# Forgetting attention: output product of one query tile joined to the scores of a later one, transposes and norm sums in other slots

## What is computed

```python
def block(inp):                       # one block of 128 queries
    q_b, c_b, start = inp
    logits = (jnp.einsum('bqhd,bkhd->bhqk', q_b, kf)
              + c_b[..., None] - c_k[:, :, None, :])
    q_pos = start + jnp.arange(Q_BLOCK)
    logits = jnp.where(key_pos[None, :] <= q_pos[:, None], logits, -jnp.inf)
    return jnp.einsum('bhqk,bkhd->bqhd', jax.nn.softmax(logits, axis=-1), vf)
...
o_fox = rms_norm(o_fox, fox_norm[i].reshape(FOX_HEADS, FOX_DH)).reshape(B, L, FOX_WIDTH)
h = h + jnp.concatenate([o_gla, o_fox], axis=-1) @ w_out[i]
```

## Time and profile before

| | before |
|---|---|
| median of 3 runs | 2259.5 us |
| profiled execution, span | 2257.8 us |
| PE busy | 2237.6 us (99%) |
| VectorE busy | 1411.1 us (62%) |
| ScalarE busy | 1049.8 us (46%) |
| chain that ended last | PE 93%, VectorE 3%, ScalarE 2% |
| granted TensorE clock | 0.999 of full |

### The profile page before, as it was taken

One profiled execution on the slowest core, in us unless ns is written; L12 is line 12 of the kernel. 1 busy time (PEld: TensorE's weight loads), 2 busy tenths in 40 slices (PEclk: granted clock), 3 DMA queues, 4 the chain that ended last, 5 costly groups with the idle time before them and its releaser, 6 DMA issues.

```text
span 2257.8 us, 39364 instructions
## 1 busy us (share of the span) xinstructions
PE 2237.6 (99%) x15807; PEld 2024.5 (90%) x15807; DVE 1411.1 (62%) x2601; ACT 1049.8 (46%) x1963; POOL 118.6 (5%) x203
## 2 busy tenths in 40 slices
PE   9999999999999999999999999999999999999998
PEld 7798999999997898999899888978899888898997
DVE  5356576759743465667689566869455455863664
ACT  5356554447633465544377443223244444552652
POOL 3001010000000001100000010101000000000001
PEclk9999999999999999999999999999999999999999
DMA  6545676245433436732355262767711122443651
GB/s 216 165 124 152 177 194 182 100 141 174 136 103 117 120 110 151 184 110 96 111 175 166 88 182 78 191 187 201 212 67 57 66 94 93 153 157 115 182 166 51
DMA packets 97112, 313.01 MB, mean 139 GB/s; under 512 B 13809, under 2 KB 17811, under 8 KB 95907
## 3 DMA queue, kind: packets, MB, share of 16 engines
q1 hardware_dynamic: 84627, 220.93, 29.6%
q0 software_dynamic: 11584, 88.25, 16.7%
q10 hardware_dynamic: 720, 1.31, 0.2%
HBM read 308.32 MB, written 86.02 MB: 175 GB/s over the span
## 4 chain that ended last, share of the span: by engine, by line
PE 93%; DVE 3%; ACT 2%; issue 1%; DMA 0%; POOL 0%; SPq 0%; ACTq 0%; DVEq 0%; POOLq 0%
PE G L1427 58%; PE G L1464 15%; PE G L1537 7%; PE X L1464 3%; PE X L1749 1%; PE X L1704 1%; PE X L1831 1%; PE X L1727 1%; DVE wL L2423 1%; PE X L1815 1%; PE X L1532 1%; ACT wH L1884 1%; PE X L1800 1%; PE X L1427 1%; PE X L1787 0%
## 5 line engine op out<-in xcount | busy, mean ns | idle before, releaser
L1884 ACT ACTIVATE wH<-raw 128x512 fp32r<-128x512 f32 (+3 forms) x693 | 475.0, 704 | 468.2 <-PE G L1427 386.9
L2423 DVE TENSOR_TENSOR wL<-raw,wH 128x512 fp32r<-128x512 f32 (+3 forms) x693 | 538.2, 788 | 240.2 <-ACT wH L1884 236.8
L1427 PE MATMUL G<-aH,wH 128*128 128x264 f32 (+2 forms) x2000 | 503.1, 317 | 2.0 <-DVE aL L2436 1.5
L1427 PE MATMUL G<-aH,wL 128*128 128x264 f32 (+2 forms) x2000 | 481.7, 306 | 0.0
L1427 PE MATMUL G<-aL,wH 128*128 128x264 f32 (+2 forms) x2000 | 481.2, 306 | 0.0
L1427 PEld LDWEIGHTS G<-aH,wH 128*128 128x128 f32 x2000 | 324.6, 189 | 28.2 <-issue 6.1
L1427 PEld LDWEIGHTS G<-aH,wL 128*128 128x128 f32 x2000 | 322.6, 188 | 17.2
L1427 PEld LDWEIGHTS G<-aL,wH 128*128 128x128 f32 x2000 | 322.6, 188 | 14.2 <-issue 0.2
L1464 PE MATMUL G<-seven,wH 128*128 128x256 f32 (+2 forms) x960 | 177.5, 284 | 1.6 <-DVE wL L2423 1.5
L2582 DVE TENSOR_TENSOR hT<-G,hT 128x528 f32<-128x528 f32 (+1 forms) x83 | 58.0, 699 | 183.4 <-PE G L1427 183.4
L1464 PEld LDWEIGHTS G<-seven,wH 128*128 128x128 f32 x960 | 148.0, 188 | 3.8 <-issue 3.0
(11 more groups left out here) (407 smaller groups left out, 3916.4 us busy)
## 6 DMA issues: line engine op xcount, KB each, us to landing
raw<-weights SPq DMA_DIRECT2D x195, 512.0 KB, 3.5
weight_sums<-weights POOLq DMA_DIRECT2D x72, 704.0 KB, 6.4
raw<-weight_sums SPq DMA_DIRECT2D x160, 256.0 KB, 2.9
raw<-weights SPq DMA_DIRECT2D x48, 704.0 KB, 4.0
raw<-weights SPq DMA_DIRECT2D x121, 256.0 KB, 2.8
weight_sums<-weight_sums POOLq DMA_DIRECT2D x24, 704.0 KB, 5.2
weight_sums<-weights POOLq DMA_DIRECT2D x24, 448.0 KB, 4.9
raw<-weights SPq DMA_DIRECT2D x12, 384.0 KB, 5.5
```

Source lines behind the costliest of these rows:

```text
L1427: done = e.matmul(m.pair(i)[0:M, bank, 0:n], a[:, k, 0:M], b[:, kx, lo - t0:lo - t0 + n], start=(k == 0 and c == 0), stop=(k == nk - 1 and ...
L1884: e.activation(m.high(i)[:, c], m.raw(i)[:, c], ACT.Copy).then_inc(s.w_hi, 1)
L2423: e.tensor_tensor(m.low(i)[:, c], m.raw(i)[:, c], m.high(i)[:, c].bitcast(F32), ALU.subtract).then_inc(s.w_lo, 1)
```

## The change

The body of the loop over w is laid out anew, and `RATE_FOX` goes from 0.8 to 0.64. `fo`(w−2) moves from the third slot of w to its first, directly ahead of `fs`(w). The first `yield` is skipped for w = 0. `ft`(w−1, 0) keeps the second slot, with `nsq` ahead of it for i = 2. `ft`(w−1, 1) moves to the third slot; for i = 2 `nsum` 0 stands ahead of it. The fourth slot holds `nsum` 1 (i = 2, so one w earlier than before) or `ft`(w−1, 2) (i = 1), then `fmeta`, `ftail` and `fn`(w, 1) as before. The extra slots that these steps had are gone, and so is the separate `nsum` 1 behind the loop.

```diff
-RATE_STATE, RATE_OUT, RATE_FOX, RATE_INDEX, RATE_HEADS = 0.5, 0.75, 0.8, 0.33, 0.62
+RATE_STATE, RATE_OUT, RATE_FOX, RATE_INDEX, RATE_HEADS = 0.5, 0.75, 0.64, 0.33, 0.62
@@ bg() in attention(l), for w in range(18) @@
                 if w < 16:
                     while ("fq", l, p) not in done:
                         yield "blocked"
+                if 2 <= w:
+                    step("fo", l, w - 2)
+                if w < 16:
                     step("fs", l, w)
                     if i == 1 and 1 <= p < 3:
                         step("sums", l, 2 * p + 2)
                         step("sums", l, 2 * p + 3)
                     if i == 4:
                         done.add(("pair", p))
-                yield
+                if w:
+                    yield
+                if i == 2 and p:
+                    step("nsq", l, p - 1)
                 if 1 <= w < 17:
                     step("ft", l, w - 1, 0)
                 yield
-                if i == 3 and p:
-                    step("nsum", l, p - 1, 1)
-                    yield
-                if 2 <= w:
-                    step("fo", l, w - 2)
+                if i == 2 and p:
+                    step("nsum", l, p - 1, 0)
                 if w < 16:
                     step("fn", l, w, 0)
-                yield
                 if 1 <= w < 17:
                     step("ft", l, w - 1, 1)
+                yield
+                if i == 2 and p:
+                    step("nsum", l, p - 1, 1)
+                if i == 1 and p:
+                    step("ft", l, w - 1, 2)
                 if i == 3 and w < 16:
                     step("fmeta", l, w)
                     if w == 10:
...
                 if w < 16:
                     step("fn", l, w, 1)
                 yield
-                if i == 1 and p:
-                    step("ft", l, w - 1, 2)
-                    yield
-                if i == 2 and p:
-                    step("nsq", l, p - 1)
-                    yield
-                    step("nsum", l, p - 1, 0)
-                    yield
-            step("nsum", l, 3, 1)
-            yield
             step("ftail", l, 3)
             done.add(("mix", 7))
```

## The result

| | before | after |
|---|---|---|
| median of 6 runs | 2259.47 us (2258.88 to 2259.78) | 2266.55 us (2265.74 to 2267.49) |
| ratio to before, 95% interval | | 1.0032 [1.0022, 1.0042] |
| profiled execution, span | 2257.8 us | 2265.1 us |
| granted TensorE clock, whole run | 0.999 | 0.998 (in all six runs) |

The change makes the kernel slower by 7.1 us, 0.32%. The forecast was 2268.7 us.

The account below looks back on a forecast made before the run. TensorE, busy 99% of the 2257.8 us span, was taken as the bound. −5.6 (joins) + 15.6 (`ft` waits) + 1.8 (dry) − 2.6 (old waits) = +9.2 us, giving 2268.7 us; range 2254 to 2276.

Parts of the forecast that it names:

- Part 1: `fo` joined to `fs`, 14 times a layer: each saves one re-entry and one entry, 0.20 us; 5.6 us in all.
- Part 3: `ft`(w−1,1) comes sooner after `fs`(w) and waits for its copy queued behind the exponentials: 7.8 us a layer, 15.6 in two.
- Part 4: Foreground runs dry before `fs`(3), so `fo`(1) waits for the copy of `ft`(1,1): 0.9 us a layer, 1.8 in two.
- Part 5: Old PE waits in the attention stretch go: 1.3 us a layer, 2.6 in two.
- `fo`(7) behind its copy: `fo`(7), one step behind `ft`(·,2), comes after 1.1 us against about 1.0 for the copy, so no wait.
- a join does nothing: Rival: each join gives 0.09 us or less while the waits come: 2271.8 us; chance 0.56 together with the forecast.
- Part 2: The other joins, `nsum` and `ft` (all full-array), cost or save zero, bounds −0.1 to +0.1 us for each of 8.
- the 0.09 behind a transposition: The foreground step after a transpose group takes 0.82 us instead of 0.73, put down to its own weight loads.
- joins win: Rival: ScalarE keeps up, no wait at `ft`, −6.4 us: 2253.1 us; chance 0.15.
- only the floor is left: Rival: foreground pieces on ScalarE mostly fall elsewhere, `ft` waits 5.4 us in place of 15.6: 2258.5 us; chance 0.22.
- the backlog: Rival: a late `ft` also delays other copies and VectorE's minima come late, +16.3 us: 2275.8 us; chance 0.07.
- The two layers behave alike, so I work one out and double it: Forgetting attention stretch: 134.30 us in either layer, clock granted in full, so one layer's terms were doubled.

Follow-up runs that it names:

- runs 1: Kernel before, old slots and rate, with only `fo`(w−2) moved directly ahead of `fs`(w): 2263.33 us.
- 11: run 9 with the `pair` mark one w earlier, RATE_FOX 0.66, and `fo` back in the third slot for i = 3 and 4: 2257.26 us.
- run 9: Changed kernel with `ft`(w−1, 1) in the fourth slot for i = 2, 3, 4 and foreground pieces held back from `fs`(w) to `ft`(w−1, 0): 2255.07 us.
- run 8: Changed kernel with `fs`(w) ahead of `fo`(w−2) and `ft`(w−1, 1) in the fourth slot for i = 2, 3, 4: 2259.28 us.
- run 4: Changed kernel with `ft`(w−1, 1) moved from the third slot to the fourth, except for i = 1: 2258.30 us.
- run 5: Changed kernel with the foreground's pieces held back between `fs`(w) and `ft`(w−1, 0), PE's order the same: 2259.11 us.
- run 2: Changed kernel with `ft`(w, 0) in the fourth slot of its own w and `ft`(w−1, 1) in the second: 2273.75 us.
- Run 3: Changed kernel with the copies of `ft`(·, 0) to PT made by VectorE instead of ScalarE: 2273.16 us.
- run 6: Changed kernel with the joined pair turned round, `fs`(w) first and `fo`(w−2) directly behind it: 2264.10 us.

## Why the prediction was right

The direction, the place and, within 2.2 us, the time were right. By the steps of the prediction, us per layer, measured by distances in layer 0:

| term | predicted | measured |
|---|---|---|
| Part 1, 14 joins | −2.8 | −2.8 |
| Part 3, waits at `ft` | +7.8 | +6.9 |
| Part 3, w = 3 / 7 / 11 | 1.46 / 1.46 / 1.94 | 1.46 / 1.56 / 2.16 |
| Part 4, dry stretch | +0.9 | +0.9 |
| Part 5, old waits | −1.3 | −2.3 |
| `fo`(7) behind its copy | 0 | +0.4 |

**Part 1** holds: the tail of `fo` stays, re-entry and entry go. By distances a join is worth 0.20 us in after, 0.18 in runs 1 and 11, 0.19 in run 9. The rival that a join does nothing falls, and run 8 against run 4 shows where it would nearly hold: with an untiled product in between. What Part 2 put at zero is not measured by itself; it is in these figures. The reason that it gives for the 0.09 behind a transposition, weight loads, no run here shows.

**Part 3** holds in its mechanism, which run 5 isolates without changing PE's order, and run 2 from the other side. Of its terms w = 4, 8, 9 and 12 were too large (0.21, 0.50, 0, 0.40 against 0.34, 0.82, 0.49, 0.58): each was the old order's lag carried over, with a guess at the pieces that fall between. Which of those failed I did not trace for each. The rivals that joins win, or that only the floor is left, fall with it; the backlog, 11 us a layer, did not come either.

**Part 4** is exact. PE's timeline of after:

```profile
150.16 0.52 PE L1724 MATMUL X<-ident,Sb 128*128 128x128 f32 x3
151.35 0.88 PE L1746 MATMUL X<-PT,fv 128*64 128x128 f32 x12 [0.67 <-ACT PT L2282]
```

1.19 us from start to start, where three transposes take 0.25 with foreground behind them: 0.94.

**Part 5** was mis-sized. I took the 1.3 us that the view of waits lists for before; by distances it was 2.3, as delays without a listed wait (0.75 at w = 11 in place of 0.60, and several of 0.1 to 0.4) count too.

Sum: −2.8 + 6.9 + 0.9 − 2.3 + 0.4 = +3.1 a layer, 6.2 in two, where 9.2 was predicted. The landmarks give 2.6 for layer 0. One yardstick for both kernels (at each entry, the distance less the usual one) gives 2.5 us of waits in before and 8.0 in after, 5.4 more without rounding; since the layer grows by 2.6, the joins and all that Part 2 moved are left with 2.8, 0.20 a join. So the half microsecond lies in the sizes of single waits in the table. Another 0.5 us arises between the two stretches (+2.39 to +2.85), and what makes it is open.

One step failed outright: "The two layers behave alike, so I work one out and double it". Layer 0 cost 2.6 us and layer 1 4.3, because in layer 1 TensorE's clock fell behind a wait, and no term had the clock in it. The measured 7.3 us of the span come nearer to the forecast than the terms do only because of these 1.6 us; that nearness is luck.

## What to carry to other kernels

Two pieces of PE work that are tiled otherwise than the bulk were worth joining for their entry and re-entry, 0.2 us a pair here, where they really touch: a full-array product at the seam takes more than half of it back. Before moving one, count the distance of every dependent pair in PE time against the chain it must cover, with all that stands in the in-order queue ahead of the copy, whatever engine has it; here the waits at `ft` were 6.9 us a layer against 2.8 for the joins. When such an order is changed, keep the distance (a later slot) and clear the queue (no background pieces between producer and copy): 2255.1 us instead of 2266.6, and 2259.4 before.

## What the runs showed of the hardware that I had not expected

The extra cost in layer 1 is TensorE's clock. Windows of after around `ft` at w = 11, layer 1 (PEclk is the column ahead of DMA share and GB/s):

```profile
868.00:871.80 3.80, 3.80 (x34) 3.24 (x30) 3.77 (x9) 1.71 (x4) 0.00 (x0) 1.00 0.87 141
871.80:874.20 2.40, 0.43 (x5) 0.34 (x4) 1.01 (x5) 1.95 (x6) 0.47 (x1) 1.00 0.39 77
...
874.60:877.90 3.30, 3.30 (x18) 3.30 (x16) 1.74 (x4) 1.08 (x2) 0.01 (x1) 0.51 0.96 245
```

and PE's timeline there:

```profile
873.89 0.63 PE L1724 MATMUL X<-ident,Sb 128*128 128x128 f32 x4 [1.97 <-ACT PT L2282]
...
875.44 0.64 PE L1424 MATMUL G<-mixH,wH 128*128 128x264 f32 x2
875.88 0.64 PE L1424 MATMUL G<-mixL,wH 128*128 128x264 f32 x2
```

After a wait of 1.97 us PE works on, and 0.7 us later the granted clock is 0.51, the lower level of 1.2 GHz, for 3.3 us; pairs start 0.44 us apart in place of 0.24. That costs some 3.3 × 0.49 = 1.6 us, which is nearly all of the difference between the layers (4.3 against 2.6). The same wait in layer 0, 2.0 us, is followed by a window at full clock:

```profile
223.70:225.70 2.00, 2.00 (x17) 2.00 (x18) 1.14 (x3) 1.12 (x2) 0.00 (x0) 1.00 0.70 87
```

Run 3 has it twice, both times in layer 1: behind its wait of 2.17 us at w = 3 the clock is near half for 3.4 us from 812.1, and behind its wait of 2.44 us at w = 11 for 3.4 us from 880.4. The same two waits in layer 0 are followed by pairs that start 0.24 apart. In run 2 it is the other way round: there the fall stands in layer 0, behind a shorter wait, and the wait of 1.71 us at the same place of layer 1 has none behind it. PE's timeline of run 2 in layer 0:

```profile
140.41 0.55 PE L1724 MATMUL X<-ident,Sb 128*128 128x128 f32 x3 [1.72 <-DVE Sb L2946]
...
143.09 0.64 PE L1424 MATMUL G<-aL,wH 128*128 128x264 f32 x2
143.53 0.64 PE L1424 MATMUL G<-aH,wL 128*128 128x264 f32 x2
```

The profiled executions of the other runs show no half clock in the stretches of either layer; the longest wait among them is 1.7 us (run 6), as long as the one of run 2.

It also differs between executions of one kernel. Of the five of run 2 only the profiled one has a mean clock of 0.998, and it takes 2275.58 us; the other four have 0.999 and take 2273.25 to 2273.91. Of the five of run 3, three have 0.997 and take 2272.9 to 2273.2 us, two have 0.996 and take 2276.3 and 2276.7. So a wait of 2 us can cost 3.6, in one place or one execution and not in another. Neither the length of the wait nor the layer decides by itself; what does is open.

The Trainium skill (TensorE: Matmul & The Clock Gate, Part 1) says that idleness throttles the clock and activity releases it. The trace agrees in that the half clock follows an idle stretch and that full clock is back while PE works on, 3.4 us later; equal waits in the other layer have no half clock behind them.
